# Issuing the three products of a weight block operand by operand over the banks instead of bank by bank

## What is computed

```python
def conv_ffn(h, w_up, dw, w_down):
    u = causal_depthwise_conv(h @ w_up, dw)          # width 3
    gate, val = jnp.split(u, 2, axis=-1)
    return (jax.nn.silu(gate) * val) @ w_down

for i in range(DEPTH):                               # DEPTH = 2
    if i % 2 == 0: y = sliding_window_sink_attention(x, wq, wk, wv, wo, sinks)
    else:          y = conformer_conv_module(x, w_in, dw, norm_g, norm_b, w_out)
    x = layer_norm(ALPHA * x + y, ...)
    y = conv_ffn(x, ffn_w_up[i], ffn_dw[i], ffn_w_down[i])
    x = layer_norm(ALPHA * x + y, ...)
```

## Time and profile before

| what | value |
|---|---|
| median of 3 runs | 2269.79 us |
| runs | 2268.48, 2269.79, 2270.3 us |
| span of the profiled execution | 2270.0 us |
| TensorE busy | 2109.4 us (93%) |
| VectorE busy | 1582.9 us (70%) |
| ScalarE busy | 1020.4 us (45%) |
| GpSimd busy | 244.6 us (11%) |
| mean granted TensorE clock | 0.959 of full speed |
| moved by DMA | 383.30 MB, mean 169 GB/s |

### The profile page before, as it was taken

How to read it: one execution, slowest core, us unless ns; L and a number is a source line. 1 busy time by engine, 2 the same in 40 slices (tenths; PEclk the granted TensorE clock), 3 DMA queues, 4 the chain that set the end, 5 groups by cost and what they waited for, 6 DMA issues and landing times.

```text
span 2270.0 us, 37362 instructions
## 1 busy us (share of the span) xinstructions
PE 2109.4 (93%) x11575; PEld 1829.5 (81%) x11575; DVE 1582.9 (70%) x2285; ACT 1020.4 (45%) x1410; POOL 244.6 (11%) x109
## 2 busy tenths in 40 slices
PE   8989989999999999998967576989999999999996
PEld 6877778888888888887967576778888888888885
DVE  5558467777677775546789999866767677775545
ACT  4456344444444443433634342544444444443433
POOL 1000010000000000001645653110000000000002
PEclk9997999999999999998988888999999999999998
DMA  7540446565656665554333322446565656666553
GB/s 240 183 145 1 153 145 192 177 201 177 200 180 193 187 230 197 193 192 157 119 114 102 111 93 93 149 151 192 177 202 178 201 179 193 191 227 236 191 193 116
DMA packets 313142, 383.30 MB, mean 169 GB/s; under 512 B 23087, under 2 KB 236127, under 8 KB 312017
## 3 DMA queue, kind: packets, MB, share of 16 engines
q1 hardware_dynamic: 311552, 373.38, 51.6%
q0 software_dynamic: 1232, 6.95, 0.9%
q10 hardware_dynamic: 288, 2.10, 0.2%
HBM read 380.24 MB, written 2.10 MB: 168 GB/s over the span
## 4 chain that ended last, share of the span: by engine, by line
PE 78%; DVE 12%; issue 7%; ACT 1%; DVEq 1%; DMA 0%; SPq 0%; ACTq 0%
PE ps L327 29%; PE ps L323 14%; PE ps L244 10%; PE ps L245 10%; PE ps L246 10%; DVE conv_out L573 6%; DVE x L640 1%; PE ps L280 1%; PE ps L282 1%; PE ps L281 1%; PE ps L1413 1%; PE ps L1425 1%; DMA x<-in_x_dram 0%; DVE w_lo L214 0%; DVEq L564 0%
## 5 line engine op out<-in xcount | busy, mean ns | idle before, releaser
L214 DVE TENSOR_TENSOR w_lo<-raw,w_hi 128x1024 fp32r<-128x1024 f32 x624 | 761.7, 1224 | 538.6 <-ACT w_hi L209 531.0
L209 ACT ACTIVATE w_hi<-raw 128x1024 fp32r<-128x1024 f32 x704 | 743.5, 1058 | 825.1 <-PE ps L246 372.2
L327 PE MATMUL ps<-xT,w_hi 128*128 128x512 f32 x2816 | 967.6, 394 | 2.4 <-DVE xT L697 2.4
L323 PE MATMUL ps<-xT,w_lo 128*128 128x256 f32 x2816 | 753.5, 278 | 0.0
L327 PEld LDWEIGHTS ps<-xT,w_hi 128*128 128x128 f32 x2816 | 516.6, 188 | 110.5 <-DVE xT L697 3.2
L323 PEld LDWEIGHTS ps<-xT,w_lo 128*128 128x128 f32 x2816 | 529.7, 188 | 15.8
L244 PE MATMUL ps<-w_hi,hT 128*128 128x512 f32 x832 | 325.3, 391 | 5.5 <-DVE hT L1321 4.2
L245 PE MATMUL ps<-w_lo,hT 128*128 128x512 f32 x832 | 324.8, 390 | 0.0
L246 PE MATMUL ps<-w_hi,hT 128*128 128x512 f32 x832 | 324.7, 390 | 0.0
L214 POOL TENSOR_TENSOR w_lo<-raw,w_hi 128x1024 fp32r<-128x1024 f32 x80 | 223.3, 2807 | 793.9 <-ACT w_hi L209 793.9
L573 DVE SCALAR_TENSOR_TENSOR conv_out<-glu,conv_taps,conv_out 128x256 f32 (+1 forms) x380 | 257.6, 734 | 8.1
(11 more groups left out here) (170 smaller groups left out, 1720.1 us busy)
## 6 DMA issues: line engine op xcount, KB each, us to landing
raw<-in_ffn_w_up_dram SPq DMA_DIRECT2D x704, 256.0 KB, 3.1
raw<-in_ffn_w_down_dram SPq DMA_DIRECT2D x352, 256.0 KB, 2.9
raw<-in_conv_w_in_dram SPq DMA_DIRECT2D x128, 256.0 KB, 2.8
raw<-in_attn_wq_dram SPq DMA_DIRECT2D x64, 256.0 KB, 2.9
raw<-in_attn_wo_dram SPq DMA_DIRECT2D x64, 256.0 KB, 2.9
raw<-in_conv_w_out_dram SPq DMA_DIRECT2D x64, 256.0 KB, 2.9
raw<-in_attn_wk_dram SPq DMA_DIRECT2D x16, 256.0 KB, 5.9
raw<-in_attn_wv_dram SPq DMA_DIRECT2D x16, 256.0 KB, 3.3
```

What stands on the lines that cost most here:

```text
L209: nc.scalar.activation(w_hi[:, slot, :], raw[:, slot, :], ACT.Copy).then_inc(hi_ready, 1)
L214: v.tensor_tensor(w_lo[:, slot, :], raw[:, slot, :], w_hi[:, slot, :].bitcast(F32), ALU.subtract).then_inc(lo_ready, 1)
L323: nc.tensor.matmul(ps[:, bank, 0:T], wl, xT[:, k, 0:T], start=False, stop=False, skip_group_check=True)
L327: mm = nc.tensor.matmul(ps[:, bank, :], wh, xT[:, k, :], start=(k == 0), stop=(k == KD - 1), skip_group_check=True)
```

## The change

In `halves` the blocks before the last four go through a new function, `paired_chunk`. For each token tile it issues hi x `w_hi` for the two banks, then hi x `w_lo` for the two banks, then lo x `w_hi` for the two banks. The wait for a bank in block k = 0 stands ahead of that bank's first product, as before. The last four blocks, and the keys, values and queries, stay as they are.

In `groups` with `cross`, each step of k issues the four products with `w_hi` (512 columns) for the four banks and then the four with `w_lo` (256 columns) for the four banks. Before, a bank's products of both steps of k came one after another, the `w_lo` product first except at k = 0. `w_in` keeps its order.

```diff
--- before.py
+++ after.py
@@ -249,19 +249,37 @@
                     mm.then_inc(bank_done, 1)
             mm.then_inc(chunks_done, 1)
 
+        def paired_chunk(pe, turn, slot, src, k, bank_free=None):
+
+            pe.wait_ge(lo_ready, turn * RING + (slot + 1))
+            for tok in range(TT):
+                hi = src[:, k, tok * P:(tok + 1) * P]
+                lo = src[:, k, T + tok * P:T + (tok + 1) * P]
+                for n in range(2):
+                    if bank_free is not None:
+                        bank_free(tok * 2 + n)
+                    nc.tensor.matmul(ps[:, tok * 2 + n, :], hi, w_hi[:, slot, n * BANK:(n + 1) * BANK],
+                                     start=(bank_free is not None), stop=False)
+                for n in range(2):
+                    nc.tensor.matmul(ps[:, tok * 2 + n, :], hi, w_lo[:, slot, n * BANK:(n + 1) * BANK],
+                                     start=False, stop=False)
+                for n in range(2):
+                    mm = nc.tensor.matmul(ps[:, tok * 2 + n, :], lo, w_hi[:, slot, n * BANK:(n + 1) * BANK],
+                                          start=False, stop=False)
+            mm.then_inc(chunks_done, 1)
+
         def halves(pe, name, src, kt, free, done, src_ready=None):
 
 
             with pe.Fori(0, 2) as h:
                 for k in range(kt - RING):
                     turn = h * (kt // RING) + (TURN[name] + k // RING)
-                    parts = [(tok * 2 + n, tok, [(k, n * BANK)]) for tok in range(TT) for n in range(2)]
                     if src_ready is not None and k % 2 == 0:
 
                         pe.wait_ge(src_ready[0], k // 2 + 1 + src_ready[1])
 
-                    rows_chunk(pe, turn, k % RING, src, parts, k == 0, False,
-                               lambda b: pe.wait_ge(free, h * (b + 1) + 1))
+                    paired_chunk(pe, turn, k % RING, src, k,
+                                 (lambda b: pe.wait_ge(free, h * (b + 1) + 1)) if k == 0 else None)
 
 
                 end = range(kt - RING, kt)
@@ -302,7 +320,18 @@
                     if j == RING and middle is not None and not (before is not None and b == 0):
                         middle(pair * 2 + b, b)
                     pe.wait_ge(lo_ready, turn * RING + (slot + 1))
-                    for m in ((0, 1, 2, 3) if cross else (2, 3, 0, 1)):
+                    if cross:
+                        for kk in range(2):
+                            k = 2 * j + kk
+                            for m in range(4):
+                                col = (m // 2) * 512 + kk * 256 + (m % 2) * P
+                                nc.tensor.matmul(ps[:, 4 * b + m, :], w_hi[:, slot, col:col + P], xT[:, k, :],
+                                                 start=(k == 0), stop=(k == KD - 1), skip_group_check=True)
+                            for m in range(4):
+                                col = (m // 2) * 512 + kk * 256 + (m % 2) * P
+                                mm = nc.tensor.matmul(ps[:, 4 * b + m, 0:T], w_lo[:, slot, col:col + P],
+                                                      xT[:, k, 0:T], start=False, stop=False, skip_group_check=True)
+                    for m in (() if cross else (2, 3, 0, 1)):
                         for kk in range(2):
                             k = 2 * j + kk
                             bank = 4 * b + m
@@ -316,18 +345,7 @@
                                                       stop=(k == KD - 1))
                                 if m == 3 and k == KD - 1:
                                     mm.then_inc(gate_done, 1)
-                                continue
-
-
-                            def low():
-                                nc.tensor.matmul(ps[:, bank, 0:T], wl, xT[:, k, 0:T],
-                                                 start=False, stop=False, skip_group_check=True)
-                            if k > 0:
-                                low()
-                            mm = nc.tensor.matmul(ps[:, bank, :], wh, xT[:, k, :],
-                                                  start=(k == 0), stop=(k == KD - 1), skip_group_check=True)
-                            if k == 0:
-                                low()
+
                     mm.then_inc(chunks_done, 1)
             group(0, 0, before)
             group(0, 1)
```

## The result

| | before | after |
|---|---|---|
| median | 2269.6 us (4 runs, 2268.48 to 2270.3) | 2282.32 us (4 runs, 2281.7 to 2282.71) |
| span of the profiled execution | 2270.0 us | 2280.2 us |

The change makes the kernel slower by a factor of 1.0046 (95% interval 1.0031 to 1.0061), +12.7 us by the medians. The forecast was 2271 and the range ended at 2280. In each later run that lists both, the time is 2.2 or 2.3 us more than the span, so by the same difference the profiled execution of before will have taken some 2272.3 us, 2.7 above its median, and the spans differ by 10.2 only.

The account below looks back on a forecast made before the run. TensorE's matmul pitch was taken as the bound. Terms of 0 (`halves` pitch), -0.6 (`groups` pitch) and +1.7 us (bank 3 wait) made +1.1, hence 2271 us; range 2265 to 2280.

Parts of the forecast that it names:

- TensorE's pitch bounds the up and down stages: In the up- and down-projections TensorE is always busy, so only the distance between matmul starts sets the time.
- Pitch in `halves`, 2,496 x 0: In `halves`, the 2,496 matmuls keep 226.7 ns each whatever the bank or stationary operand order: 0 us.
- The wait for bank 3, +1.7 us: At four half boundaries, block k = 0 asks for bank 3 two matmuls earlier and stalls: +0.45 at wo, +0.41 at down0.
- Pitch in `groups`, -0.6 us: In the up-projections a block stays 2.773 us; only the dearer first block of each group gets cheaper, 44 x 13 ns.
- its upper end of +4.1: Upper bound for pitch in `groups`: if neighbours of one width are what costs, 308 more blocks pay it.
- a slower rhythm of the mixed widths: Rival: up-projection groups settle at 353.3 ns a pair instead of 346.6, +18.0 us, 2289 with the bank wait; chance 0.12.
- The sign of being wrong: Prediction wrong if a group's or block's period moves by more than 0.5%, or the bank wait is missing.
- The clock: Rival: cycling the banks drops TensorE's clock to its low level in 1% of dense matmul, 2285 us; chance 0.03.
- Same-bank accumulation: Rival: same-bank accumulation was costing 3.3 ns on each of 8,128 matmuls, so spacing banks gives -27 us, 2244; chance 0.07.
- cheap repeats: Rival: in `halves`, 832 more repeats of the stationary operand each shed 13.3 ns, -11 us, 2260; chance 0.04.
- The 0.2 us between profile and median: The profiled execution's span of 2270.0 us was taken to stand 0.2 above the median of the runs shown.

Follow-up runs that it names:

- run of eight: Against the kernel before, each up-projection block issues all eight 512-column products over four rotating banks, then all eight 256-column ones; 2281.29 us, one run.
- 320-wide product: Up-projections in the new order, `w_lo` products 320 columns wide instead of 256, otherwise the kernel before; 2355.19 us, one run.
- spaced alternation: Against the kernel before, up-projections still alternate 256 and 512 columns, but the 256 goes to the bank two further on; 2285.06 us, 1.0063.

## Why the prediction was wrong, point by point

- **TensorE's pitch bounds the up and down stages.** Right. No other engine's work changed, and the loss that the account finds is in start-to-start distances and four waits.
- **Pitch in `halves`, 2,496 x 0.** Right: 226.7 ns in the changed kernel, and no more than before once the first block is restored.
- **The wait for bank 3, +1.7 us.** Right in place, mechanism and size: stalls of 0.57 and three of 0.28 us (0.57 and 0.29 forecast), +1.6 us in all.
- **Pitch in `groups`, -0.6 us.** This is the step that failed, and with it the forecast. I added up the pitch of a pure run of 512s and that of a pure run of 256s, and took runs of four as near to pure ones, "since the long pure runs are nearer to the new runs of four than a lone pair is". A run of four isn't: in the run of eight the first five 512s behind a change of width are slow, and in the runs of four of up0 all four are (230, 231, 236 and 228 ns for 226.7). The term was +8.7 us between the two profiles, 9.2 with the first group of each stage, over its upper end of +4.1. That end priced like neighbours by a group's first block, whose pairs of equal width are runs of two; runs of four cost twice as much a block (27 to 33 ns for 13).
- **The rival "a slower rhythm of the mixed widths"** is what came, at half of its full price and in rhythms that hadn't been seen before: 2.800 and 2.807 us a block are 350.0 and 350.8 ns a pair, between the 346.6 and the 353.3 of the earlier trace rows. Rows 7 and 8 had shown that one order has two paces, and they deserved more than 0.12: the sum of pitches from pure runs is the fastest pace that any order here reached, so the new order could meet it or lie above it, but not gain.
- **The sign of being wrong** that it named, a group's period moving by more than 0.5%, came: 22.40 and 22.45 for 22.20 us are 0.9 and 1.1%. The other, a missing bank wait, didn't.
- **The clock.** 1.00 throughout the same stretches. The Trainium skill ("TensorE: Matmul & The Clock Gate", section "A second HAM failure mode: psum-queue depth-cycling") tells of a kernel whose clock swings while it cycles through banks; here the bank changes at every matmul of `groups` and the granted clock stays at 1.00 from 378.60 to 850.00.
- **Same-bank accumulation, cheap repeats.** Both fell: with one width, new and old order take 29.01 and 29.02 us a group, and a stationary operand loaded four times running costs 226.7 ns each time.
- **The 0.2 us between profile and median** was wrong in a small way: the profiled execution was about 2.7 us above the median, since a time holds some 2.3 us around the span. The forecast rested on the median in the end, so it moved little.

What stays open is what inside TensorE makes the rhythm. The weight load's spare time is not it, as far as a 320-wide product can tell, and the slow steps behind the stall of down0 point the same way, since there every load has a 512 to run beside. Why one more matmul flips a group wasn't followed further.

## What to carry to other kernels

Where matmuls of two widths alternate, the sum of the pitches measured in runs of one width was a lower bound for the mixture in every order tried here, and not its price; read the period of a whole loop body off the trace, and treat an order that shows two paces as one that a reordering can tip. Rotating PSUM banks under back-to-back accumulations was worth nothing here, and what it did cost (1.6 us) came from asking for a late bank two matmuls earlier: before moving a bank's first product forward, look up when its reader lets it go. By its time alone one variant, the spaced alternation, would have put the blame on the banks; the periods inside its trace showed that it doesn't lie there.

## What the runs showed of the hardware that was not expected

- The same sequence of 512- and 256-column matmuls, at granted clock 1.00 and with nothing to wait for, ran in two paces, 346.7 and about 353 ns a pair. In the spaced order one added matmul of 0.12 us at a group's start moved it from the slow to the fast one.
- After a change from 256 to 512 columns, in runs of eight, five matmuls pay 1 to 9 ns each over 226.7, and the first two 256s after 512s cost 114 and 119 for 120. Four 512s behind a stall pay the same (236, 228, 232 and 231 ns), with no change of width.
- At granted clock 1.00 a matmul in a pure run costs 13.3 ns more than its columns, at either width (226.7 and 120.0). The Trainium skill ("TensorE: Matmul & The Clock Gate", section "Back-to-back issue gap") gives 2.5 ns on top of the columns for a matmul by itself; with a weight load before each, the streams here never went below 13.3 on the mean of a block at that clock. At granted clock 0.50 nothing is on top: three matmuls of w_out take 1.28 us, 426.7 ns each, which is 512 columns at 1.2 GHz.
